# Decoder layer: half of the memory keys' projection between the weighted sums of the second attention

## What is computed

```python
# h: (256, 1024); mem_n = layer_norm(mem): (256, 1024)
dq, dk, dv, mq, mk, mv = split(h @ w_in)              # six projections of 512 columns
out_a = differential_attention(rope(dq), rope(dk), dv)  # "first attention", 4 heads x 2 maps
out_b = moba_attention(rope(mq), rope(mk), mv)          # "second attention", 8 heads, causal over 256
h = LN1(alpha * h + [out_a ; out_b] @ w_out)            # "mix"
q = h @ w_q;  k, v = split(mem_n @ w_kv)                # k: the memory keys, v: the memory values
h = LN2(alpha * h + softmax(q k^T / 16) v @ w_o)        # 4 heads of 256
h = LN3(alpha * h + moe(h))                             # 32 experts, top 4, each w1 (1024x2048), w2 (1024x1024)
```

## Time and profile before

| | |
|---|---|
| median of 3 runs | 1188.49 us (1187.78 to 1190.10) |
| profiled execution, own time | 1189.85 us |
| its span, first to last instruction | 1188.0 us |
| TensorE busy | 1094.0 us (92%) |
| VectorE busy | 321.6 us (27%) |
| ScalarE busy | 255.7 us (22%) |
| mean granted TensorE clock | 0.979 of full |
| DMA | 445.64 MB, mean 375 GB/s |

### The profile page before, as it was taken

How to read it: one execution, slowest core, us unless ns; L and a number is a source line. 1 busy time by engine, 2 the same in 40 slices (tenths; PEclk the granted TensorE clock), 3 DMA queues, 4 the chain that set the end, 5 groups by cost and what they waited for, 6 DMA issues and landing times.

```text
span 1188.0 us, 16129 instructions
## 1 busy us (share of the span) xinstructions
PE 1094.0 (92%) x6597; PEld 534.0 (45%) x6597; DVE 321.6 (27%) x726; ACT 255.7 (22%) x416; POOL 9.1 (1%) x14
## 2 busy tenths in 40 slices
PE   7999999999999999999999988888888888888895
PEld 5788899883333333343333333333333333333331
DVE  4986576553111111221111111111111111111114
ACT  3575645412111111111111111111111111111110
POOL 0000000000000000000000000000000000000000
PEclk9999799979999999999999999999999999999998
DMA  8756487578899999999999999999999999999994
GB/s 283 278 172 229 148 289 251 213 283 328 370 426 429 427 429 428 429 428 429 429 428 429 429 429 428 430 427 429 429 428 429 428 429 428 429 429 428 427 428 169
DMA packets 49597, 445.64 MB, mean 375 GB/s; under 512 B 5536, under 2 KB 6176, under 8 KB 24896
## 3 DMA queue, kind: packets, MB, share of 16 engines
q1 hardware_dynamic: 49568, 445.23, 91.0%
HBM read 444.16 MB, written 1.05 MB: 375 GB/s over the span
## 4 chain that ended last, share of the span: by engine, by line
PE 61%; DMA 22%; SPq 7%; DVE 4%; ACT 4%; issue 1%; another core or an unknown queue 1%; POOL 0%; DVEq 0%; ACTq 0%
PE bank L904 25%; DMA ring<-in_w_mlp 21%; PE bank L933 13%; SPq L435 6%; PE bank L546 3%; PE bank L548 3%; PE bank L547 3%; PE bank L845 3%; PE bank L836 3%; DMA w_raw<-in_w_in 1%; DVE w_low L1214 1%; ACT live L1185 1%; ACT live L1154 1%; PE bank L892 1%
## 5 line engine op out<-in xcount | busy, mean ns | idle before, releaser
L904 PE MATMUL bank<-ring,live 128*64 128x512 f32 x2048 | 458.4, 598 | 41.6 <-DMA ring<-in_w_mlp 41.6
L904 PEld LDWEIGHTS bank<-ring,live 128*64 128x64 f32 x2048 | 143.0, 137 | 338.2 <-issue 247.4
L933 PE MATMUL bank<-ring,live 128*64 128x512 f32 x1024 | 230.2, 603 | 22.0 <-ACT live L1185 22.0
L1582 DVE TENSOR_SCALAR live<-bank 128x256 f32<-128x256 f32 x64 | 24.2, 420 | 739.8 <-PE bank L904 739.8
L933 PEld LDWEIGHTS bank<-ring,live 128*64 128x64 f32 x1024 | 71.5, 138 | 158.6 <-issue 130.5
L1181 ACT ACTIVATE live<-live 128x512 f32<-128x512 f32 x32 | 20.1, 629 | 463.2 <-DVE live L1582 463.2
L1214 DVE TENSOR_TENSOR w_low<-w_raw,w_high 128x1024 fp32r<-128x1024 f32 x64 | 75.4, 1220 | 25.3 <-ACT w_high L997 25.1
L997 ACT ACTIVATE w_high<-w_raw 128x1024 fp32r<-128x1024 f32 x64 | 65.4, 1056 | 33.8 <-DMA w_raw<-in_w_in 15.9
L1187 ACT ACTIVATE live<-bank 128x512 f32<-128x512 f32 x32 | 19.1, 597 | 233.4 <-PE bank L933 233.4
L845 PE MATMUL bank<-live 64*128 64x512 f32 x256 | 63.6, 615 | 0.7 <-ACT live L1187 0.7
L836 PEld LDWEIGHTS bank<-pick,live 128*128 128x128 bf16 x1536 | 46.7, 98 | 23.6 <-issue 23.5
(11 more groups left out here) (197 smaller groups left out, 874.2 us busy)
## 6 DMA issues: line engine op xcount, KB each, us to landing
ring<-in_w_mlp SPq DMA_DIRECT2D x192, 2048.0 KB, 48.1
w_raw<-in_w_in SPq DMA_DIRECT2D x24, 512.0 KB, 8.4
w_raw<-in_w_mem_kv SPq DMA_DIRECT2D x16, 512.0 KB, 4.2
w_raw<-in_w_mix_out SPq DMA_DIRECT2D x8, 512.0 KB, 5.8
w_raw<-in_w_mem_q SPq DMA_DIRECT2D x8, 512.0 KB, 4.1
w_raw<-in_w_mem_o SPq DMA_DIRECT2D x8, 512.0 KB, 4.8
h<-in_x SPq DMA_DIRECT2D x4, 256.0 KB, 5.3
mem_o<-in_mem SPq DMA_DIRECT2D x2, 512.0 KB, 8.8
```

Source lines behind the costliest of these rows:

```text
L904: mm = pe.matmul(up[n][64 * g:64 * g + SLOTS, :], x_e[:, k, :], slot(at)[:, col:col + 512], start=False, stop=(k == KC - 1))
L933: mm = pe.matmul(ty[64 * g:64 * g + SLOTS, :], hidT[:, P * c + 64 * u:P * c + 64 * u + SLOTS], slot(at)[:, D * c + 512 * g:D * c + 512 * ( ...
```

## The change

The blocks of weights come in another order: block 0 of the memory keys (`kv` 0, now block 8, units 32 to 35) before the two mix blocks (now 9 and 10, units 36 to 43), then `kv` 1 as before (block 11). TensorE does `kmT` 0 one chunk after each of the first six weighted sums and two chunks after the last, ahead of the `oT` transposes; `kmT` 1 takes the place that `kmT` 0 had, with four chunks ahead of the first `h1T` tile, three ahead of the second and one behind it. `kmT` 0 holds four banks through the second attention, and the other jobs there share the remaining four. `plan_banks` now gives each job the bank that was given out longest ago. `cs` moves behind the first scores. ScalarE copies `vm` block 1 ahead of the high parts of `oT` and has its splits moved around; VectorE's order changes at the `split` counts.

```diff
-BLOCKS = [("in", b) for b in range(6)] + [("kv", 2), ("kv", 3), ("out", 0), ("out", 1), ("kv", 0), ("kv", 1),
+BLOCKS = [("in", b) for b in range(6)] + [("kv", 2), ("kv", 3), ("kv", 0), ("out", 0), ("out", 1), ("kv", 1),
 def plan_banks():
+    def take(names, allowed=range(8)):
+        for name in names:
+            b = next(b for b in by_age if b in allowed)
+            by_age.remove(b)
+            by_age.append(b)
+            plan[name] = (b, used[b])
+            used[b] += 1
...
+    take(tiles("Tmq") + tiles("Tmk") + tiles("vm", 0) + [("S", m) for m in range(8, 16)] + tiles("vm", 1))
+    take([("kmT", 0, j) for j in range(4)])
+    free = [b for b in range(8) if b not in [plan["kmT", 0, j][0] for j in range(4)]]
+    take([("TA", 4), ("oT", 0, 0), ("oT", 1, 0)], free)
     for m in range(4, 12):
+        take(([("TA", m + 1)] if m < 11 else []) + [("PV", m)], free)
+    take([("oT", 0, 1), ("oT", 1, 1)], free)
+    take(tiles("mix", 0) + tiles("mix", 1))
+    take([("h1T", t, q) for t in range(NT) for q in range(2)])
+    take([("kmT", 1, j) for j in range(4)])
...
@@ TensorE
                 weigh(j)
+                if j < 10:
+                    project_cols(8, left_m, "kmT", 0, chunks=[j - 4])
+            project_cols(8, left_m, "kmT", 0, chunks=[6, 7])
             pe.wait_ge(o_ready, 2)
             for t in range(NT):
                 turn_rows("oT", mem_o, t, 1)
-            project_rows(8, left, (("mix", 0, 0), ("mix", 0, 1)), turned_rows("oT"))
-            project_rows(9, left, (("mix", 1, 0), ("mix", 1, 1)), by_tile=True)
-            project_cols(10, left_m, "kmT", 0)
-            for t in range(NT):
+            project_rows(9, left, (("mix", 0, 0), ("mix", 0, 1)), turned_rows("oT"))
+            project_rows(10, left, (("mix", 1, 0), ("mix", 1, 1)), by_tile=True)
+            for t in range(NT):
+                project_cols(11, left_m, "kmT", 1, chunks=[range(0, 4), range(4, 7)][t])
                 for q in range(2):
                     pe.wait_ge(ln_ready, 4 + 2 * t + q + 1)
                     turn_rows("h1T", h, t, q)
-            project_cols(11, left_m, "kmT", 1)
+            project_cols(11, left_m, "kmT", 1, chunks=[7])
@@ ScalarE
             copy_probs(4)
+            copy_vm(1)
             split_rows("oT", left, BY_HALF[0:NT])
-            copy_vm(1)
...
+            split(1)
             split_rows("oT", left, BY_HALF[NT:])
-            split(6)
+            split(1)
+            copy_cols("kmT", 0, kmT)
+            split(4)
             bias_part(0)
             split(6)
-            copy_cols("kmT", 0, kmT)
@@ VectorE
             split_rows("oT", left, BY_HALF[NT:])
             split(4)
             first_halves(2, "mix")
-            split(1)
+            split(5)
             finish(2, "mix", 0, 64)
             split(3)
             finish(2, "mix", 1, 64)
-            split(4)
             split_rows("h1T", left, BY_TILE)
```

More of the change, by code:

```diff
@@ L123, in plan_banks @@
[L123 to L133, removed]
@@ L135, in plan_banks @@
-    assert sorted(plan["mo", 1, t][0] for t in range(NT))[0] >= 4
-    late = [(("rT", 0, 0), 0), (("rT", 1, 0), 1), (("rT", 0, 1), 2), (("rT", 1, 1), 3), (("lg", 0), 0), (("lg", 1), 1),
-            (("rank", 0), 2), (("rank", 1), 2)]
-    for name, b in late:
-        plan[name] = (b, used[b])
-        used[b] += 1
+    plan, used, by_age = {}, [0] * 8, list(range(8))
+    def take(names, allowed=range(8)):
[5 more added lines that the diff above has]
+            used[b] += 1
@@ new lines, in tiles @@
+    def tiles(*name):
+        return [name + (t,) for t in range(NT)]
+    take([("xT", t, 0) for t in range(NT)] + tiles("dq") + [("xT", t, 1) for t in range(NT)])
+    take(tiles("dk") + tiles("dv") + tiles("Tdq") + tiles("Tdk"))
+    take([("memT", t, q) for t in range(NT) for q in range(2)])
+    take([("S", m) for m in range(8)] + [("cs",)])
+    take(tiles("mq") + tiles("mk") + tiles("mv"))
+    take([("TA", 0), ("TA", 1), ("PV", 0), ("TA", 2), ("PV", 1), ("TA", 3), ("PV", 2), ("PV", 3)])
@@ new lines, in plan_banks @@
+    take([("kmT", 1, j) for j in range(4)])
+    take([("qmT", 0, j) for j in range(4)] + [("MS", 0), ("MS", 1)])
+    take([("qmT", 1, j) for j in range(4)] + [("TP", 0), ("TP", 1), ("MS", 2), ("MS", 3)])
+    take([("PM", 0), ("TP", 2), ("PM", 1), ("TP", 3), ("PM", 2), ("PM", 3)])
+    take(tiles("mo", 0))
+    take(tiles("mo", 1), range(4, 8))
+    for name, b in ((("rT", 0, 0), 0), (("rT", 1, 0), 1), (("rT", 0, 1), 2), (("rT", 1, 1), 3), (("lg", 0), 0), (("lg", 1), 1),
+                    (("rank", 0), 2), (("rank", 1), 2)):
+        take([name], [b])
@@ L325, in decoder_layer @@
         last_job = [("dq", 1), ("dk", 1), ("dv", 1), ("mq", 1), ("mk", 1), ("mv", 1), ("vm", 0, 1), ("vm", 1, 1),
-                    ("mix", 0, 1), ("mix", 1, 1), ("kmT", 0, 3), ("kmT", 1, 3), ("qmT", 0, 3), ("qmT", 1, 3),
+                    ("kmT", 0, 3), ("mix", 0, 1), ("mix", 1, 1), ("kmT", 1, 3), ("qmT", 0, 3), ("qmT", 1, 3),
                     ("mo", 0, 1), ("mo", 1, 1)]
@@ L573, in project_rows, with project_cols @@
                             mm.then_inc(unit_used, 1)
-            def project_cols(blk, act_, name, cb, before=None):
+            def project_cols(blk, act_, name, cb, before=None, chunks=range(KC)):
                 b = [bank_for(pe, name, cb, j) for j in range(4)]
-                for c in range(KC):
+                for c in chunks:
                     u = UNITS * blk + c // 2
@@ L1403, in _ @@
             split(4)
+            split_rows("memT", left_m, BY_TILE)
+            mask_group(0)
+            split(2)
+            mask_group(1)
             b = wait_filled(dve, "cs")
```

31 lines of the change are left out of this document (5 added, 26 removed).

## The result

| | median | runs |
|---|---|---|
| kernel before, measured beside it | 1188.70 us | 1187.78 to 1190.10 (4) |
| changed kernel | 1201.26 us | 1198.70 to 1204.48 (4) |

The ratio is 1.0108 with a 95% interval of 1.0083 to 1.0132: the changed kernel is 9.9 to 15.7 us slower. The forecast was 1202.0. The profiled execution of the changed kernel took 1203.12 us (span 1201.2) against 1189.85 before.

The account below looks back on a forecast made before the run. The DMA bounds the expert loop, a nearly closed TensorE chain the dense stage. 1189.85 + 5.6 (13.2 of new waits less 7.6) + 7.9 for the clock = 1203.4, against the median 1202.0 us; range 1192 to 1209.

Parts of the forecast that it names:

- W5: Start of `qmT` 0: new wait for unit 48, behind the low parts of all four `h1T` banks; 1.3 us.
- W3: Start of `mix` 1: new wait for unit 40, which stands behind `first_halves` on VectorE; 3.3 us.
- W1: Start of the second attention: new wait for the second `oT` bank, held by ScalarE's `vm` block 1 copy; 1.5 us.
- (c): Expert loop: DMA-bound, it swallows the delay, so no change, 1188.5 us; chance 0.07.
- (d): Second attention: unit 40's load comes earlier in a DMA hole, 3.7 us won, so faster, 1184.8 us; chance 0.06.
- (e): Dense stage: bank plan or VectorE's order doesn't hold TensorE where forecast; 1190.5 or 1183.6 us; chance 0.05.
- W2: Start of `mix` 0: new wait for unit 36, which VectorE makes behind the low parts of `oT`; 2.9 us.
- The clock: Behind the five new waits: falls of the granted clock, charged 7.9 us in all, bounds 0 and about 14.
- W4: Start of `kmT` 1: new wait for `mix` 1's tile 1 bank, drained behind `finish` and three units; 4.2 us.
- (a): New waits: the clock holds through them, so only +5.6 us, about 1193.5 us; chance 0.14.
- (b): Second attention: the clock goes back and forth all through it, about +6 to the forecast, 1208 us; chance 0.12.
- Taken away, 7.6: Second attention and mix blocks: two waits 1.8 us, slow clock 5.2 and 0.6 us, together 7.6 us saved.

Follow-up runs that it names:

- the delay put in: Kernel before with 54 unused matmuls of 512 columns between `mix` 1 and `kmT` 0: 1197.22 us, ratio 1.0106.
- in one piece: Kernel with all five new waits taken away, but `kmT` 0 run whole behind the last weighted sum: 1191.23 us, ratio 1.0031.
- `cs` alone: Kernel before with only `cs` moved behind the first scores: 1187.15 us, ratio 0.9992.
- the kernel at 1182.3: Changed kernel with the causes of all five new waits taken away by other orders and banks: 1182.31 us, ratio 0.9954.
- clock kept: Changed kernel with 12, 13 and 17 unused matmuls inside its three longest waits: 1194.96 us, ratio 1.0060.

## Why the prediction held, step by step

The time was 1201.3 for 1202.0. That it came so near is in part luck: misses of its terms (W5 and W3's clock too small, W1's clock too large, the first stage 0.4 us better than charged) set each other off. The mechanism held, and two terms of it need a correction, as said below:

- **End = start of `qmT` 0, one for one:** right. Foretold near 202, it was 200.77; the table above and the delay put in show the slope. Rivals (c) and (d) fall with it.
- **W1 to W5:** 1.5, 2.9, 3.3, 4.2 and 1.3 foretold, 1.35, 2.93, 3.19, 4.08 and 1.82 found. Rival (e) falls. On W2 I had named VectorE's unit 36, with ScalarE's copies of `kmT` 0 done 0.3 us sooner. The profile names ScalarE (147.82 + 1.21 = 149.03), and unit 36 was done at about 147.81 + 1.17 = 148.98: a tie, so I moved both. W5 is the one mis-sized term: unit 48 ended at 200.40, but `qmT` 0 began at 200.77, and with unit 48 out of the way 0.51 us of "issue" still stood there. I had put 0.1 for it.
- **The clock:** foretold 7.9, found 9.0. W3's 3.1 against 1.9 is the miss (a stretch of 6.83 us, of which only the beginning lies in the wait); W4's 2.4 against 2.1, W2's 1.9 against 1.5 and W5's 1.6 against 1.2 are near, and W1's 1.2 didn't come. Rival (a) falls by the kernel in which the waits stay and the clock is kept.
- **Rival (b):** falls. The second attention ran at 1.00 in every profile of a kernel with chunks between its sums, W1 or no W1. What I had set beside it (the Trainium skill, TensorE: Matmul & The Clock Gate, "A second HAM failure mode: psum-queue depth-cycling") blames the short idle times that come with cycling through PSUM banks. Cycling alone didn't do it here: the sums went round four banks at 1.00, and with the pause filled even thin sums alone kept the clock. The stretches seen in this part of the kernel all stood behind an idle time, of 1.08 us (two of four) or 1.95 us (in one piece).
- **Taken away, 7.6:** right in this pair of profiles, and its reason was half right. I had blamed thin sums "with waits just before". With the pause of 1.08 us filled by four useless matmuls the same thin sums kept the clock, and even with the pause the loss does not come in every execution: two of the four profiled executions with this code (before, twice; `cs` alone; the delay) had it. Medians of the kernel before contain it, as the drop of 4.4 us to the median of the filled kernel shows.
- **First stage, 0:** right (0.9992), though not as told. The wait became 1.61 and 0.27, the projection began at 58.56 (58.95 before; foretold 57.9), the slow stretch was gone and not shifted. In three other kernels with these waits it was there.

The added waits outweigh what was won because each of them was set by an order written for the old place of the blocks. VectorE and ScalarE did the same work in the same sequence, but the units in it now belonged to an earlier step of TensorE, and the four banks of `kmT` 0 had been the slack that hid `finish`.

## What to carry to other kernels

When a block of TensorE's work is moved to fill its gaps, go through the other engines' queues for the step that now comes first: what unit, copy or drain does it need, and what stands ahead of that there? As it stood, the change cost 12.6 us by the medians; it gained (3.3 to 7.6 us by the ratio) only when those orders and the bank plan moved with it, as they did in the kernel at 1182.3. And before an idle pause is filled with real work, try it with a few useless matmuls. Four of them gave 0.26% (0.07 to 0.44%) here without any block moved; since they leave the length of the pause and take away only the slow clock, they tell what real work in the same place can gain beyond them, in this case 0.4 us in the profiles.

## What the hardware showed beyond that

**A short pause brings the slow clock in some executions and not in others.** Counted over the fourteen profiled executions, for pauses of TensorE of 0.67 us and more at these steps (up to the memory scores):

| pause | where | stretch at 0.50 behind it or begun in it |
|---|---|---|
| 0.67 to 0.76 us | memory scores | 0 of 14 |
| 0.67 and 0.87 us, then 0.27 | first stage, clock kept | 0 of 1 |
| 1.08 us | second head, sums behind it | 2 of 4, 13.65 us each |
| 1.31 to 1.35 us | second `oT` bank | 0 of 6 |
| 1.45 or 1.61 us, then 0.27 | first stage | 3 of 9, 3.41 us each |
| 1.82 us | `qmT` 0 | 6 of 6, 3.41 us |
| 1.95 us | second head, in one piece | 1 of 1, 17.07 us |
| 2.46 us | first stage | 4 of 4, 3.41 us |
| 2.93 us | `mix` 0 | 4 of 5, 3.41 or 6.83 us |
| 3.19 us | `mix` 1 | 5 of 5, 3.41 or 6.83 us |
| 4.08 us | `kmT` 1 | 5 of 5, 3.41 or 6.83 us |

**And what follows the pause sets how long it stays slow.** Behind 1.08 us among the sums it was 13.65 us (17.07 behind 1.95 in the kernel in one piece), while with dense matmuls behind the pause 1.00 was back after 3.41 or 6.83. The shortest pause that brought a stretch, 1.08 us, thus had a dearer one, some 5 us, than any in dense work (at most 3.1). In the router, which no experiment touched, 13.65 us at 0.50 stand in every profile among thin work with pauses under 1 us, while 0.67 to 0.76 us ahead of the memory scores brought none in fourteen; so the length of the pause alone doesn't decide. What in an execution decides whether the clock falls stays open.
